# Three quads of modulation vectors summed on GpSimd in a two-layer transformer kernel

## What is computed

```python
silu_c = jax.nn.silu(c)
silu_cctx = jax.nn.silu(c_ctx)
for i in range(DEPTH_2):            # two layers
    sh1, sc1, g1, sh2, sc2, g2 = jnp.split((silu_c @ mod_w[i] + mod_b[i])[:, None, :], 6, axis=-1)
    a_lat = modulate(rms_norm(h_lat, norm_mix_g[i]), sh1, sc1)
    ...
    csh1, csc1, cg1, csh2, csc2, cg2 = jnp.split(silu_cctx @ mod_w[i] + mod_b[i], 6, axis=-1)
```

## Time and profile before

| | |
|---|---|
| median of 3 executions | 1858.08 us (1855.1 to 1861.33) |
| profiled execution | 1856.31 us, span 1854.5 us |
| mean granted TensorE clock | 0.974 |
| busy: TensorE, VectorE, ScalarE, GpSimd | 1714.5, 1116.1, 566.0, 581.6 us |

### The profile page before, as it was taken

One profiled execution on the slowest core, in us unless ns is written; L12 is line 12 of the kernel. 1 busy time (PEld: TensorE's weight loads), 2 busy tenths in 40 slices (PEclk: granted clock), 3 DMA queues, 4 the chain that ended last, 5 costly groups with the idle time before them and its releaser, 6 DMA issues.

```text
span 1854.5 us, 24573 instructions
## 1 busy us (share of the span) xinstructions
PE 1714.5 (92%) x9694; PEld 1321.5 (71%) x9694; DVE 1116.1 (60%) x2065; ACT 566.0 (31%) x905; POOL 581.6 (31%) x570
## 2 busy tenths in 40 slices
PE   7999999998879889799879888999999999999999
PEld 6876688775537356566546556979999745579997
DVE  4344357877787887767787667555553125635554
ACT  4443433211121212111211114333332244734332
POOL 0111101767667676467766660000000100000000
PEclk9998999999999999899979999999999999999999
DMA  8998885999999999999999995835555223035553
GB/s 274 321 325 278 282 270 190 407 409 409 409 395 396 409 409 408 392 370 407 408 409 409 409 401 174 279 114 182 181 182 164 90 64 105 1 108 188 181 182 135
DMA packets 223419, 515.91 MB, mean 278 GB/s; under 512 B 13324, under 2 KB 122204, under 8 KB 223324
## 3 DMA queue, kind: packets, MB, share of 16 engines
q0 software_dynamic: 86784, 318.80, 44.4%
q1 hardware_dynamic: 136192, 195.71, 30.8%
q10 hardware_dynamic: 348, 0.11, 0.0%
HBM read 513.53 MB, written 1.05 MB: 277 GB/s over the span
## 4 chain that ended last, share of the span: by engine, by line
PE 60%; DMA 22%; DVE 7%; POOL 5%; issue 3%; ACT 2%; SPq 0%; DVEq 0%; POOLq 0%
DMA more<-in_peer_v_dram,idx 14%; PE bank L911 9%; PE bank L914 9%; PE bank L912 9%; DMA more<-in_peer_u_dram,idx 5%; POOL more L806 5%; PE bank L1273 4%; PE wide L1325 4%; PE bank L865 4%; PE wide L1060 2%; DVE more L2430 2%; PE wide L1551 1%; DMA weights<-in_w_in_dram 1%; PE bank L1505 1%; PE bank L987 1%
## 5 line engine op out<-in xcount | busy, mean ns | idle before, releaser
L2039 DVE TENSOR_TENSOR low_weights<-weights,high_weights 128x2048 fp32r<-128x2048 f32 x102 | 233.6, 2292 | 302.7 <-ACT high_weights L1660 302.3
L2430 DVE CUSTOM_DVE_ANT_0 more<-more,wide 128x1024 f32<-128x1024 f32 x256 | 310.8, 1219 | 153.4 <-DMA more<-in_peer_u_dram,idx 151.5
L911 PE MATMUL bank<-high_input,high_weights 128*128 128x256 f32 x1216 | 346.4, 285 | 7.8 <-DVE low_input L2039 6.7
L912 PE MATMUL bank<-high_input,low_weights 128*128 128x256 f32 x1248 | 351.5, 282 | 0.0
L806 POOL DMA_INDIRECT more<-in_peer_u_dram,idx x256 | 283.5, 1107 | 200.9 <-DVE dots L2430 91.6
L914 PE MATMUL bank<-low_input,high_weights 128*128 128x256 f32 x1216 | 344.1, 283 | 0.0
L1325 PE MATMUL wide<-more,rstd 128*128 128x512 f32 x476 | 242.0, 644 | 78.9 <-ACT rstd L1848 60.2
L1660 ACT ACTIVATE high_weights<-weights 128x2048 fp32r<-128x2048 f32 x102 | 195.2, 1915 | 312.7 <-DMA weights<-in_ffn_w_gate_dram 86.9
L806 POOL DMA_INDIRECT more<-in_peer_v_dram,idx x256 | 252.5, 986 | 116.0 <-issue 70.2
L1273 PE MATMUL bank<-nrm,weights 128*128 128x256 f32 x1088 | 242.3, 381 | 1.0 <-DVE big L2039 1.0
L1273 PEld LDWEIGHTS bank<-nrm,weights 128*128 128x128 f32 x1088 | 208.7, 192 | 48.2 <-issue 21.6
(11 more groups left out here) (287 smaller groups left out, 2323.1 us busy)
## 6 DMA issues: line engine op xcount, KB each, us to landing
weights<-in_ffn_w_down_dram SPq DMA_DIRECT2D x33, 1024.0 KB, 5.0
weights<-in_ffn_w_gate_dram SPq DMA_DIRECT2D x30, 1024.0 KB, 5.4
weights<-in_ffn_w_up_dram SPq DMA_DIRECT2D x30, 1024.0 KB, 5.3
weights<-in_conv_w_in_dram SPq DMA_DIRECT2D x24, 1024.0 KB, 8.9
weights<-in_w_in_dram SPq DMA_DIRECT2D x20, 1024.0 KB, 9.5
nrm<-in_mod_w_dram POOLq DMA_DIRECT2D x14, 1024.0 KB, 8.0
sq<-in_mod_w_dram POOLq DMA_DIRECT2D x13, 1024.0 KB, 6.9
h_ctx<-in_mod_w_dram POOLq DMA_DIRECT2D x13, 1024.0 KB, 6.5
```

Of the source, the lines that this page charges most:

```text
L911: first = nc.tensor.matmul(out, cut(high), hi, start=start, stop=False, **more_args)
L912: nc.tensor.matmul(out, cut(w_lo[b]), hi, start=False, stop=False, **more_args)
L2039: return nc.vector.tensor_tensor(out, a, b, op)
L2430: nc.vector.tensor_tensor_reduce(u, u, wide[0][:, :], 1.0, 0.0, ALU.mult, ALU.add, dots[:, n % 16:n % 16 + 1]).then_inc(s_dot, 1)
```

## The change

The twelve chunks 32 to 43 (`POOL_MODS`), quads 8, 9 and 10, are multiplied and added by GpSimd. It loads two chunks ahead, 32 to 39 into the `nrm` and `sq` buffers, 40 to 43 into those in `more` and `big`, with two loads at a time outstanding. For each chunk it multiplies both row blocks in place by the conditioning value of each partition (two `tensor_scalar`) and adds them into `pool_sum` (one `tensor_tensor` for the first chunk of a quad, two for the others); every instruction waits for the one before it (`settle`). That makes 24 `tensor_scalar` and 21 `tensor_tensor`, all 128 x 1024. `cvec[:, k, 0:1]` is the column of `c`; the sums are those for `c`.

TensorE then sums the 128 partitions of a quad with four matmuls (`mod_sum`) whose stationary side `pick` has ones in one column. The sum of quad 8 stands where chunk 39 stood, that of quad 9 where chunk 40 stood, that of quad 10 where chunk 43 stood. The turn of quad 8 moves from behind chunk 37 to ahead of the sum of quad 9. ScalarE's copies of the rows follow the sums.

```diff
+POOL_MODS = list(range(32, 44))
 LATE_MODS = list(range(40, 44))
-LATE_BUFFER = dict(zip(LATE_MODS, [0, 1, 0, 1]))
+SUM_AT = {39: 8, 40: 9, 43: 10}
...
 def turned_after(j):
 
+    late = {37: [], 40: [8]}
+    if j in late:
+        return late[j]
     return [(j - 5) // MOD_PARTS] if j >= 5 and j % MOD_PARTS == 1 else []
...
+        pool_sum = [h_ctx[:, :, :].rearrange("p k t -> p (k t)")[:, 0:D], view(more, 16896, D)]
+        pick = view(top_scratch, 0, 2, 32)
...
+            settle(nc.gpsimd.memset(pick, 0.0))
+            for v in range(2):
+                settle(nc.gpsimd.memset(pick[:, v, v:v + 1], 1.0))
+
+            for j in range(POOL_MODS[0]):
...
+            own_w = [mod_w[0], mod_w[1], late_w[0], late_w[1]]
+
+            def load_own(j):
+
+                if j < POOL_MODS[2]:
+                    pool.wait_ge(s_mod_used, j - 1)
+                if j == LATE_MODS[0]:
+                    wait_emptied(pool, "pair", HALVES // 2 - 1)
+                nc.gpsimd.dma_start(own_w[own(j)], mod_source(j)).then_inc(pool_landed[own(j)], 16)
+
+            def sum_own(j):
+
+                quad, part = j // MOD_PARTS, j % MOD_PARTS
+                first = LATE_MODS[0] if j >= LATE_MODS[0] else POOL_MODS[0]
+                pool.wait_ge(pool_landed[own(j)], 16 * ((j - first) // 2 + 1))
+                total = pool_sum[quad // 10]
+                if part == 0 and quad == 9:
+                    pool.wait_ge(s_mod_used, mods_used(39))
+                rows = [own_w[own(j)][:, k, :] for k in range(2)]
+                for k in range(2):
+                    settle(nc.gpsimd.tensor_scalar(rows[k], rows[k], cvec[:, 2 * part + k, 0:1], None, ALU.mult))
+                if part == 0:
+                    settle(nc.gpsimd.tensor_tensor(total, rows[0], rows[1], ALU.add))
                 else:
-                    nc.gpsimd.dma_start(mod_w[j % 3], src).then_inc(m_landed[j % 3], 16)
+                    settle(nc.gpsimd.tensor_tensor(rows[0], rows[0], rows[1], ALU.add))
+                    settle(nc.gpsimd.tensor_tensor(total, total, rows[0], ALU.add))
+                if part == MOD_PARTS - 1:
+                    pool.sem_inc(s_pool_sum, 1)
+
+            pool.wait_ge(s_cvec, 3)
+            load_own(32)
+            load_own(33)
+            for j in POOL_MODS:
+                sum_own(j)
+                if j + 2 < LATE_MODS[0] or j >= LATE_MODS[0] and j + 2 in POOL_MODS:
+                    load_own(j + 2)
+                if j == 37:
+                    load_own(40)
+                    load_own(41)
...
+            def mod_sum(quad):
+
+                pe.wait_ge(s_pool_sum, quad - POOL_MODS[0] // MOD_PARTS + 1)
+                pe.wait_ge(s_mod_left, quad)
+                for v in range(2):
+                    for half in range(2):
+                        rows = slice(32 * (2 * v + half), 32 * (2 * v + half) + 32)
+                        mm = nc.tensor.matmul(sbank[3][rows, :], pick[:, v, :], pool_sum[quad // 10][:, 512 * half:512 * half + 512],
+                                              start=True, stop=True)
                 mm.then_inc(s_mod_used, 1)
...
             def mods(j):
 
-                mod_chunk(j)
+                if j < POOL_MODS[0]:
+                    mod_chunk(j)
                 for quad in turned_after(j):
                     mod_turn(quad)
+                if j in SUM_AT:
+                    mod_sum(SUM_AT[j])
```

More of the change, by code:

```diff
@@ L53, with mods_used @@
 MOD_QUADS = 2 * MODS // MOD_PARTS
+POOL_MODS = list(range(32, 44))
 LATE_MODS = list(range(40, 44))
-LATE_BUFFER = dict(zip(LATE_MODS, [0, 1, 0, 1]))
+SUM_AT = {39: 8, 40: 9, 43: 10}
 BUBBLE_MODS = list(range(44, 48))
-def late_landed(j):
-    return 16 * sum(1 for m in LATE_MODS if m <= j and LATE_BUFFER[m] == LATE_BUFFER[j])
+def mods_used(j):
+    if j in SUM_AT:
+        return POOL_MODS[0] + list(SUM_AT).index(j) + 1
+    return j + 1 if j < POOL_MODS[0] else j + 1 - len(POOL_MODS) + len(SUM_AT)
 def chunk_name(c):
@@ L147, in scores_of @@
     return SECOND if g == 1 else g // 2
-MIXES = [("turn_ctx", _g) for _g in range(4)] + mod_turns(41) + [("mix", 0), ("mixnorm_ctx", 0), ("mix", 1), ("mix", 2), ("mix", 3)]
+MIXES = mod_turns(40) + [("turn_ctx", _g) for _g in range(4)] + mod_turns(41) + [("mix", 0), ("mixnorm_ctx", 0), ("mix", 1), ("mix", 2), ("mix", 3)]
 CONV_OUTS = [("conv_out_lat", 0), ("mixnorm1_ctx", 0)] + [("conv_out_lat", _s) for _s in range(1, 4)]
@@ L401, in program @@
         part_f = view(top_scratch, 160, 2, TOPK)
-        pick = view(top_scratch, 192, 2, TOPK)
+        picked = view(top_scratch, 192, 2, TOPK)
         chosen = view(top_scratch, 224, TOPK)
@@ L510, in program @@
         s_last_mod = sem("second_gate_copied")
-        late_landed_at = [sem(f"late_modulation_weights_landed{j}") for j in range(2)]
+        pool_landed = [sem(f"pool_modulation_weights_landed{j}") for j in range(4)]
+        s_pool_step = sem("pool_modulation_step")
+        s_pool_sum = sem("pool_modulation_summed")
         s_sq_free = sem("squares_free")
@@ L778, in _, with mod_source @@
         def _(pool):
[L781 to L794, removed]
+            def mod_source(j):
                 quad, part = j // MOD_PARTS, j % MOD_PARTS
@@ L797, in _, with settle @@
                 at = D * (quad % (MOD_QUADS // 2))
-                src = mv[:, 2 * part:2 * part + 2, at:at + D]
-                if late:
-                    nc.gpsimd.dma_start(late_w[LATE_BUFFER[j]], src).then_inc(late_landed_at[LATE_BUFFER[j]], 16)
-                else:
-                    nc.gpsimd.dma_start(mod_w[j % 3], src).then_inc(m_landed[j % 3], 16)
+                return mv[:, 2 * part:2 * part + 2, at:at + D]
+            stepped = [0]
+            def settle(instruction):
+                stepped[0] += 1
+                instruction.then_inc(s_pool_step, 1)
+                pool.wait_ge(s_pool_step, stepped[0])
@@ new lines, in _, with own @@
+            settle(nc.gpsimd.memset(pick, 0.0))
+            for v in range(2):
+                settle(nc.gpsimd.memset(pick[:, v, v:v + 1], 1.0))
+            for j in range(POOL_MODS[0]):
+                if j == 1:
+                    pool.wait_ge(s_sq_free, 1)
+                if j >= 3:
+                    pool.wait_ge(s_mod_used, j - 2)
+                nc.gpsimd.dma_start(mod_w[j % 3], mod_source(j)).then_inc(m_landed[j % 3], 16)
+            def own(j):
+                return 2 + j % 2 if j >= LATE_MODS[0] else j % 2
@@ L1699, in mod_rows @@
             def mod_rows(j):
-                quad = j // MOD_PARTS
-                if j % MOD_PARTS == MOD_PARTS - 1:
-                    act.wait_ge(s_mod_used, j + 1)
+                quad = SUM_AT.get(j, j // MOD_PARTS)
+                if j in SUM_AT or j % MOD_PARTS == MOD_PARTS - 1 and j not in POOL_MODS:
+                    act.wait_ge(s_mod_used, mods_used(j))
                     if quad >= 2:
@@ L1775, in _ @@
                     nc.scalar.activation(x_hi[:, here, :], gate[:, here, :], ACT.Copy).then_inc(s_mix_hi, 1)
+            mod_rows(40)
             leaves("turn_ctx", 4, h_ctx)
@@ L2340, in pair @@
                 settle(tt(eq, eq, top_f[:, b].unsqueeze(1).to_broadcast([P, TOPK, TOPK]), ALU.mult))
-                settle(nc.vector.tensor_reduce(pick[:, b], eq, AX.X, ALU.add))
+                settle(nc.vector.tensor_reduce(picked[:, b], eq, AX.X, ALU.add))
             def share(g):
```

7 lines of the change are left out of this document (3 added, 4 removed).

## The result

| | before | after |
|---|---|---|
| median | 1859.7 us (1855.1 to 1861.82) | 1916.57 us (1911.0 to 1918.3) |
| profiled execution, span | 1856.31, 1854.5 us | 1915.19, 1913.4 us |
| mean granted clock | 0.974 | 0.954 |

The account below looks back on a forecast made before the run. GpSimd was to become the bound, TensorE leading the chain before: +3.8 us undisturbed, 22 from VectorE's two-input operations, making +25.8, plus 2 for the clock: +28 on 1856.3, 1885 as median; range 1861 to 1902.

Parts of the forecast that it names:

- The first step of the argument: At the sum of quad 8, TensorE, relieved of chunks, could arrive at 216.7 and waits for GpSimd, which ends last.
- the loss of clock behind the last sum: Behind the sum of quad 10, TensorE's wait could halve its clock over mix 2 and 3: 0 to 6.6 us, 2 taken.
- The undisturbed price of a sum: GpSimd's two-input tensor_tensor of 128x1024: 2.3 us, between 1.8 and 2.7; 21 make 48.3.
- The sum at the end of the prediction: Whole kernel: 25.8 + 2 = +28 us on 1856.3, median 1.8 higher, so 1885 after rounding.
- tensor_scalar, one tensor in ... I take 1.05 us; 24 make 25.2: GpSimd's products in quads 8 to 10, priced from the nearest rows, memset and copy: 1.05 us each, 25.2 in all.
- the forecast of 304.6 for the end of quad 10: GpSimd finishes summing quad 10 at 304.6: 282.6 undisturbed plus 22 us of waiting for VectorE.
- held by VectorE: From 199 to 279, VectorE's 26.1 us of two-input operations hold GpSimd for about 0.85 of that: 22 us.
- rival C: GpSimd's operations dearer than the rows say, or VectorE's chain held over 15 us: 1893 to 1910; chance 0.15.
- the "up to 15 us" of the prediction: Before mix 0, VectorE's chain, if held in turn by GpSimd, becomes up to 15 us longer.
- Rival D: Quads 8 to 10: GpSimd keeps up and TensorE's relief is kept, gain 8.8 us, 1849; chance 0.10.
- If GpSimd were never late, the place of chunk 43 would come 10.1 us earlier: At the sum of quad 10, TensorE's relief from removed chunks and waits: 10.1 us earlier, at 268.7.
- T8: Time quad 8 is summed; TensorE's own path reaches the sum of quad 10 at T8 + 52.0.

## Why the prediction was half of the loss

The first step of the argument held. TensorE stood before the sum of quad 8 at 214.77 (forecast 216.7; it was already 1.96 us ahead at chunk 30, before any edited instruction), and waited there for GpSimd; GpSimd ended last at every sum; the loss of clock behind the last sum is 1.8 us (fetch 40.8 after that sum, 39.0 before), forecast 2; the rest of the kernel ran as long as before. The 2 was partly luck: its ground was a short wait, and the wait was 27.37 us. The undisturbed price of a sum, 2.3, is 2.34 in the trace. The Trainium skill's figure (GPSIMD Engine Reference, Elementwise - side-by-side cycle accounting) halved gives an estimate of 2.25, and the trace agrees within 0.1 us. The sum at the end of the prediction is 1 us short: 1856.3, 27.8 and 1.8 are 1885.9.

**The step that failed is "tensor_scalar, one tensor in ... I take 1.05 us; 24 make 25.2".** The product took 2.85 us, so the 24 took 45 us more than forecast. Against the forecast of 304.6 for the end of quad 10, by terms read from the timeline:

| term | forecast | measured | difference |
|---|---|---|---|
| first product starts | 199.0 | 194.3 | -4.7 |
| 24 products, with 0.08 between | 1.05 each | 2.93 | +45.1 |
| 21 sums, with 0.08 between | 2.3 | 2.42 | +2.5 |
| held by VectorE | 22 | 9.9 | -12.1 |
| loads, waits, rest | | | +0.9 |

The sum is +31.7, so 336.3. The first load was issued 1.7 us earlier than before (188.51 against 190.21), since TensorE was ahead there: its granted clock from 158 to 172 us was 0.63, and 0.51 before. It landed after 5.7 us, not 8.8; before, a third load was issued at 188.22, which the change doesn't have. The 9.9 is busy time above the undisturbed: 3.4 in products (71.8 less 24 x 2.85) and 6.5 in sums (55.6 less 21 x 2.34). Quad 8 alone looks well forecast, 238.2 against 234, and that is luck: its eight products took 15 us more, and contention less than 1 us of the 7 put down for it. The mistake was to take fill and copy as the nearest rows for anything with one tensor in. Those rows showed no arithmetic, so the upper bound should have been as wide as for the sum, and rival C, which had a dearer product at 1.5 us, was the right mechanism with a bound too low. A product at 2.7 us there would have made +40. That the read of the operand is not the cause is shown by the constant (2.77 us); why this operation is slower than tensor_tensor is open.

**The contention was mis-sized the other way**, and partly in the wrong place. I counted all of VectorE's two-input time as GpSimd's loss. In the change VectorE is the one that loses: 31 us more busy time against 9.9 on GpSimd. I had written that no row shows VectorE held, and had counted that only for its chain before mix 0; it is held, behind mix 0 as well, where L2124's 3.26 became 8.93. The Trainium skill (SBUF - State Buffer, SBUF: two separate sides) has the pair of ports held for a whole instruction by whoever starts first. The trace agrees in both directions and in three details: the operand from PSUM frees VectorE (0.68), a fill leaves its two-input operations alone (0.69) but not VectorE's tensor_scalar (0.27 us each became 1.2; the same section counts VectorE's faster modes among the holders of the lock whatever GpSimd does), and shorter GpSimd instructions hold it for less. That this tensor_scalar runs in a faster mode is read from its length, 0.27 us for 256 elements against 0.41 for L2124's; no run changed the mode. In the change that costs little, because TensorE waits for GpSimd anyway: removing all reads brings the last sum 11.1 us forward, near the 9.9 (the median falls by 14.8, the span of the profiled execution by 8.8). Where GpSimd isn't the bound it costs more: for quad 10 alone 15.2 us at mix 0 (48.6 less 33.4), the "up to 15 us" of the prediction, and 18 us in the whole (the medians with and without the reads, 1874.99 and 1856.77); the 3 us behind mix 0 were not taken apart.

**Rival D rested on a relief that was not there.** "If GpSimd were never late, the place of chunk 43 would come 10.1 us earlier": with no arithmetic that place came at 278.45, 0.4 us earlier. The prediction carried TensorE's own path as a fixed 52 us from T8 on; it holds a transfer, and the transfer takes longer when the loads of chunks fall on it. D's own extreme, no arithmetic at all, gives 1857 and not 1849 while the loads go out as early as they can; with them held it gives 1848. So D needed a condition on the loads that it didn't name. The forecast was not hurt, since GpSimd was far from keeping up.

## What to carry to other kernels

Price a GpSimd operation by its own row, never by a fill or copy: here a multiplication by a per-partition scalar (2.85 us) was 2.9 times the memset and 1.5 times the same product written as tensor_tensor with a broadcast. Work moved to GpSimd takes from VectorE too wherever both read SBUF; look at what VectorE does there, and whether its operand could come from PSUM. And before counting relief on one engine, run the kernel with the moved work left out: if that doesn't gain, something behind it is the bound, here a transfer.

## What had not been expected

- tensor_scalar with fp32 on GpSimd costs 2.49 ns an element, more than the sum of two tensors (2.1).
- Beside fills VectorE's tensor_scalar of 256 elements is held (1.2 instead of 0.27 us), its two-input operations are not.
- The half clock at 158 us of the profile before is not in every build's execution. In that of the kernel before with held loads, the wait in the same place is 1.81 instead of 2.58 us, the granted clock stays at 1.00, and the out products start 6.4 us earlier, before any edited instruction; the median is no better. The run without arithmetic and with held loads has 1.00 there too, the other runs between 0.55 and 0.88. So a difference of a few us between single traces can lie ahead of the edit; times counted from the start of the out products leave that part out. Windows of before, then of that kernel (us; busy PE, PEld, DVE, ACT, POOL; PEclk, DMA share, GB/s):

```profile
158.00:172.00 14.00, 13.60 (x59) 9.32 (x60) 8.21 (x13) 3.92 (x9) 1.43 (x2) 0.51 0.82 268
```

```profile
158.00:172.00 14.00, 14.00 (x110) 9.36 (x110) 7.78 (x13) 5.25 (x11) 2.14 (x3) 1.00 0.95 318
```
